# A fourth of the weights' low parts subtracted on GpSimd instead of VectorE, in two passes of a trunk kernel

## The chip, the core and the metric

The kernel runs on one core of a Trainium2 chip. TensorE (PE) multiplies, VectorE (DVE) and ScalarE (ACT) do elementwise work, GpSimd (POOL) is a fourth compute engine, and SyncE (SP) issues the DMAs. Each engine runs its own instructions in order, and they wait for each other by semaphores. The metric is the device time of one execution in microseconds (us), lower is better.

## The reference

A trunk of two layers over 256 tokens of width 2048. Layer 0 mixes with pooling windows, layer 1 with a gated recurrence; each is followed by a SwiGLU feed-forward network (FFN) of hidden width 5632. Norms are modulated by vectors made from a conditioning vector and a large matrix `w_ada`. Cut to what the change touches:

```python
cond = jax.nn.silu(c)
for layer in range(DEPTH):                                   # 2
    mod = cond @ w_ada[layer] + b_ada[layer]                 # 2048 x 12288 each
    sh_m, sc_m, g_m, sh_f, sc_f, g_f = jnp.split(mod[:, None, :], 6, axis=-1)
    h = rms_norm(x, norm_mix_gain[layer]) * (1.0 + sc_m) + sh_m
    ...                                                      # y: pooling or recurrence
    x = x + g_m * y
    h = rms_norm(x, norm_ffn_gain[layer]) * (1.0 + sc_f) + sh_f
    a, b = jnp.split(h @ w_ffn_in[layer], 2, axis=-1)        # 2048 x 11264
    x = x + g_f * ((jax.nn.silu(a) * b) @ w_ffn_out[layer])  # 5632 x 2048
return rms_norm(x, final_gain)
```

## The kernel before

**Products.** Every float32 product is made of three with shorter operands. A weight W is split into a high part (`w_hi`, fp32r) and a low part `w_lo = W - w_hi`; activations are split in the same way into `h_hi` and `h_lo`. TensorE computes hi x hi, hi x lo and lo x hi into one PSUM buffer (lines L548, L549, L550).

**Pairs.** Weights stream from HBM in pairs of blocks, one `raw` tile of 128 x 2 x 512 each (512 KB), 696 pairs in all. A pair n passes through four stages: SP loads it into slot n mod 4 of `raw` (`load_w`, L362); ACT copies it to `w_hi` slot n mod 4 once the load has landed and TensorE has used pair n-4 (`hi`, L859, semaphore `hi_ready`); DVE subtracts (`lo`, L1165, semaphore `lo_ready`); TensorE multiplies two steps of six matmuls of 512 columns (`segment`) and counts `w_used`. SP may load pair n+4 into the slot when the low part of pair n is made.

**Passes of the first FFN.** The product with `w_ffn_in` is cut along its 2048 input features. The first pass takes features 0 to 511 for 9 column blocks of the gate half and 9 of the value half, 18 chunks of two pairs. The second pass takes features 512 to 1023 for the same 18. A pass has 36 pairs. Later passes take the rest. Chunks write alternately to PSUM buffers `prod0` and `prod1`; a chunk can begin when the one two before it has been taken out. In the first pass ACT takes them out to `part_gate` and `part_value` (L957); in the second DVE adds PSUM to these (`add_quarter`, L1464). 

**Beside them.** The vectors from `w_ada` are made in the background: SP loads blocks of 128x1024 into `ada` (L385, L387), DVE multiplies each by a column of the conditioning vector and adds it to `acc` (`fold`, L1211 and L1214). A table of spans (`BEHIND`) says at which steps these loads and folds stand, and code on each engine walks the same steps, so every engine's order is fixed when the program is written: at a step DVE does `lo`, then `add_quarter` or other callbacks, then folds. In the two passes a fold comes at about three of four pairs. SP's order is a pair's load and then the ada loads due.

GpSimd makes constants at the start, then waits (L503) for the first FFN's end before it makes constants for the recurrence.

Of the kernel before, what the change touches and what calls it, by code (L numbers as in the profile page):

```python
# [9 lines left out]
ALU = mybir.AluOpType  # L10
# [30 lines left out]
def build(nc, x, c, norm_mix_gain, norm_ffn_gain, w_ada, b_ada, pool_w, pool_scale, hgrn_w_in,  # L41
# [9 lines left out]
    HG = CH // P  # L51
# [4 lines left out]
    RAW = 4  # L56
    SPL = 4
# [3 lines left out]
    NA = 9  # L61
# [19 lines left out]
    C_M0 = C_A0 + 2 * NA  # L81
    C_B0 = C_M0 + 2 * NA
# [10 lines left out]
    START = [sum(STEPS[:n]) for n in range(len(STEPS) + 1)]  # L93

    def pairs_through(chunk):

        return (START[chunk + 1] + (WFIRST if chunk == C_WOUT else 0)) // 2
# [64 lines left out]
    with ctx:  # L162
        def sb(name, shape, dt=F32, where=ctx):
            return where.enter_context(nc.sbuf_tensor(name, shape, dt))

        def sem(name):
            return ctx.enter_context(nc.semaphore(name))
# [19 lines left out]
        raw = sb("raw", [P, RAW, 2, CH])  # L187
        w_hi = sb("w_hi", [P, SPL, 2, CH], F32R)
        w_lo = sb("w_lo", [P, SPL, 2, CH], F32R)
# [88 lines left out]
        hi_ready = sem("hi_ready")  # L278
# [11 lines left out]
        orstd_ready = sem("orstd_ready")  # L290

        lo_ready = sem("lo_ready")
        unit_summed = sem("unit_summed")
        cols_ready = sem("cols_ready")
        lb_max = sem("lb_max")
# [31 lines left out]
        def evacuated(eng, chunk):  # L327
            eng.wait_ge(prod_free[chunk % 2], chunk // 2 + 1)

        def multiplied(eng, chunk):  # L330
            eng.wait_ge(w_used, pairs_through(chunk))

        def ada_buffer(slot):
            return ada[:, slot] if slot < ADA else ada_head[:, slot - ADA]

# [18 lines left out]
        def _(sp):  # L354
            t = Tally()

            def load_w(src):
                n = t.get("raw")
                slot = n % RAW
                if n >= RAW:  # L360
                    sp.wait_ge(lo_ready, n - RAW + 1)
                sp.dma_start(raw[:, slot], src.rearrange("(a p) n -> p a n", p=P)).then_inc(raw_loaded[slot], 16)  # L362
                t.tick("raw")

# [40 lines left out]
            for src in (c, norm_mix_gain, norm_ffn_gain, hgrn_norm_gain, hgrn_lb):  # L405
                n = src.shape[0] * KD
# [20 lines left out]
            for s in range(0, AHEAD, 2):  # L427
                load_w(w_ffn_in[0, s * P:(s + 2) * P, 0:CH])
# [43 lines left out]
        @block.gpsimd  # L472
        def _(pool):
            pool.memset(ident[:, :], 0.0).then_inc(consts, 1)
            pool.memset(ones[:, :], 1.0).then_inc(consts, 1)
            pool.memset(zero[:, :], 0.0).then_inc(consts, 1)
            pool.wait_ge(consts, 3)
            pool.affine_select(out=ident[:, :], in_=ident[:, :], compare_op=ALU.not_equal, fill=1.0,
                               base=0, pattern=[[-1, P]], channel_multiplier=1).then_inc(consts, 1)
            pool.memset(fours[:, :], 0.0).then_inc(fours_begun, 1)  # L480
            for q in range(P // SQUARE):
                pool.wait_ge(fours_begun, q + 1)
                pool.affine_select(out=fours[:, :], in_=fours[:, :], compare_op=ALU.not_equal, fill=1.0, base=-q * SQUARE,
                                   pattern=[[-1, SQUARE]], channel_multiplier=1).then_inc(fours_begun, 1)

            for n, w in enumerate(WINDOWS):
                pool.memset(band[:, n], 1.0 / w).then_inc(band_begun, 1)
            pool.wait_ge(band_begun, NCH)
            for n, w in enumerate(WINDOWS):
                for at in range(w - 1):  # L490
                    pool.memset(band[:, n, 0, at:at + 1], 1.0 / (at + 1)).then_inc(band_begun, 1)
            pool.wait_ge(band_begun, N_BANDS - 4 * NCH)
            pieces = [(n, w, band[:, n, blk:blk + TB - blk // 2].rearrange("p a c -> p (a c)"), (TB - blk // 2) * P)
                      for n, w in enumerate(WINDOWS) for blk in (0, 2)]
            for _, _, m, cols_of in pieces:
                pool.affine_select(out=m, in_=m, compare_op=ALU.is_ge, fill=0.0, base=0,
                                   pattern=[[1, cols_of]], channel_multiplier=-1).then_inc(band_begun, 1)
            pool.wait_ge(band_begun, N_BANDS - 2 * NCH)
            for _, w, m, cols_of in pieces:
                pool.affine_select(out=m, in_=m, compare_op=ALU.is_ge, fill=0.0, base=w - 1,  # L500
                                   pattern=[[-1, cols_of]], channel_multiplier=1).then_inc(band_begun, 1)

            multiplied(pool, C_H - 1)  # L503
            pool.memset(keep[:, :], 1.0).then_inc(hgrn_consts, 1)
            pool.memset(masks[:, :, :], 1.0).then_inc(hgrn_consts, 1)
            pool.memset(kdec[:, :, :, :], 0.0).then_inc(hgrn_consts, 1)
            pool.wait_ge(hgrn_consts, 3)
            pool.memset(keep[:, :].rearrange("p (n c) -> p n c", c=P)[:, :, 0:1], 0.0).then_inc(hgrn_consts, 1)

            for j, h in enumerate(LEVELS):  # L510
                m = masks[:, j, :].rearrange("p (b o) -> p b o", o=h)
                pool.affine_select(out=m, in_=m, compare_op=ALU.is_ge, fill=0.0, base=0,
                                   pattern=[[-2 * h, P // (2 * h)], [0, h]], channel_multiplier=1).then_inc(hgrn_consts, 1)
            pool.wait_ge(hgrn_consts, 4 + len(LEVELS))
            for j, h in enumerate(LEVELS):
                m = masks[:, j, :].rearrange("p (b o) -> p b o", o=h)
                pool.affine_select(out=m, in_=m, compare_op=ALU.is_ge, fill=0.0, base=h - 1,
                                   pattern=[[2 * h, P // (2 * h)], [0, h]], channel_multiplier=-1).then_inc(hgrn_consts, 1)

        @block.tensor  # L520
        def _(pe):
            t = Tally()
# [9 lines left out]
            def segment(chunk, hi, lo, first, n, after=None, before=None, begin=True, end=True):  # L532

                par = chunk % 2
                if begin and chunk >= 2:
                    evacuated(pe, chunk - 2)
                for s in range(n):
                    if before is not None:
                        before(s)
                    g, k = t.get("step"), first + s  # L540
                    slot = g // 2 % SPL
                    wh, wl = w_hi[:, slot, g % 2], w_lo[:, slot, g % 2]
                    if g % 2 == 0:
                        pe.wait_ge(lo_ready, g // 2 + 1)
                    for tb in range(TB):
                        ts = slice(tb * P, (tb + 1) * P)
                        o = prod[par][:, tb]
                        pe.matmul(o, hi[:, k, ts], wh, start=(begin and s == 0), stop=False)  # L548
                        pe.matmul(o, hi[:, k, ts], wl, start=False, stop=False)  # L549
                        mm = pe.matmul(o, lo[:, k, ts], wh, start=False, stop=(end and s == n - 1))  # L550
                    if g % 2:
                        mm.then_inc(w_used, 1)
                    t.tick("step")
                    if after is not None:
                        after(s)
                    for u, (_, last) in SPAN.items():
                        if g == last + SUM:
                            reduce_unit(u)
# [9 lines left out]
            def multiply_loads(u):  # L568
                pe.wait_ge(unit_taken, u)
                n_rows, _ = folded(u)  # L570
                for k in range(n_rows):
                    n = u * KD + k
                    slot, _ = ada_slot(n)
                    ada_arrived(pe, n)
                    for o in range(2):
                        mm = pe.matmul(modp[:, o], cond_rows[:, k], ada_buffer(slot)[:, o * CH:(o + 1) * CH], start=(k == 0),  # L576
                                       stop=(in_columns(u) and k == n_rows - 1))
                    mm.then_inc(ada_free[slot], 1)
# [579 lines left out]
        def _(dve):  # L1158
            t = Tally()

            def lo():
                n = t.get("pair")
                r, slot = n % RAW, n % SPL
                dve.wait_ge(hi_ready, n + 1)
                dve.tensor_tensor(w_lo[:, slot], raw[:, r], w_hi[:, slot], ALU.subtract).then_inc(lo_ready, 1)  # L1165
                t.tick("pair")

            def ahead():
                for _ in range(AHEAD // 2):
                    lo()  # L1170
# [558 lines left out]
```

## Time and profile before

| | us |
|---|---|
| median of 3 runs | 2229.06 |
| lowest, highest | 2228.64, 2233.13 |
| the profiled execution | 2226.98 |
| its span, first to last instruction | 2225.3 |
| TensorE busy | 2164.4 (97%) |
| DVE busy | 1659.8 (75%) |
| ACT busy | 996.2 (45%) |
| POOL busy | 17.0 (1%) |

The profile is of one execution. Times count from the span's start. Busy is time with an instruction in progress; weight loads (PEld) run beside matmuls. The chain of waits is followed back from the last instruction, at each step to what released it. A window cuts the span, and waits are put down to the instruction that ended them.

### The profile page before, as it was taken

Reading aid. Unit: us, or ns where it says so; the run is one execution under the profiler, and the core shown is the slowest. Engines: PE = TensorE matmul, PEld = TensorE weight load, DVE = VectorE, ACT = ScalarE, POOL = GpSimd, SP = SyncE. Lnnn points to the kernel's source line nnn. Section 1 sums busy time; section 2 is a strip of 40 time slices with the busy share of each in tenths; the row PEclk is TensorE's granted clock in tenths of the full one; section 3 lists DMA queues with packets and bytes.
Section 4 is the critical chain, followed back from the end, with each engine's and each line's share of the span. In section 5 each row is a group of like instructions: output and inputs, shape, how many; then the busy total and the mean of one; then the engine's idle time right before and its main releaser. Section 6 shows DMA issues by size and latency. Waiting matters only on the chain.

```text
span 2225.3 us, 25178 instructions
## 1 busy us (share of the span) xinstructions
PE 2164.4 (97%) x9785; PEld 1757.7 (79%) x9785; DVE 1659.8 (75%) x1695; ACT 996.2 (45%) x1114; POOL 17.0 (1%) x77
## 2 busy tenths in 40 slices
PE   7998999999999999899999999989999999999997
PEld 4556887888888888788888888878888888888886
DVE  5768899999988876578787888667755678456644
ACT  3224544444444444464645455544454444444433
POOL 1000000000000000100000000000000000000000
PEclk9998999999999999999999999999999999999999
DMA  9998998989899886476656664568856687668664
GB/s 384 418 413 306 330 333 307 316 323 315 318 338 315 319 301 231 141 237 203 213 170 208 199 199 141 179 237 305 301 182 188 189 269 254 184 191 292 237 195 147
DMA packets 250067, 574.37 MB, mean 258 GB/s; under 512 B 17526, under 2 KB 17718, under 8 KB 249180
## 3 DMA queue, kind: packets, MB, share of 16 engines
q1 hardware_dynamic: 249948, 572.77, 75.3%
q8 instruction: 77, 1.26, 0.2%
q14 instruction: 42, 0.34, 0.0%
HBM read 570.60 MB, written 2.10 MB: 257 GB/s over the span
## 4 chain that ended last, share of the span: by engine, by line
PE 87%; DVE 3%; issue 2%; ACT 0%; DVEq 0%; ACTq 0%
PE prod L548 27%; PE prod L550 27%; PE prod L549 27%; PE small L786 2%; PE small L619 1%; DVE acc L1214 1%; PE small L760 0%; PE modp L610 0%; DVE part_value L1464 0%; PE small L799 0%; PE small L772 0%; DVE part_gate L1464 0%; PE modp L583 0%; PE small L798 0%; PE small L781 0%
## 5 line engine op out<-in xcount | busy, mean ns | idle before, releaser
L859 ACT ACTIVATE w_hi<-raw 128x1024 fp32r<-128x1024 f32 x696 | 736.4, 1061 | 1026.0 <-PE prod L550 936.2
L1165 DVE TENSOR_TENSOR w_lo<-raw,w_hi 128x1024 fp32r<-128x1024 f32 x696 | 848.4, 1223 | 432.6 <-ACT w_hi L859 430.9
L548 PE MATMUL prod<-w_hi,h_hi 128*128 128x512 f32 x2080 | 823.6, 396 | 5.8 <-issue 2.8
L550 PE MATMUL prod<-w_hi,h_lo 128*128 128x512 f32 x2080 | 811.6, 390 | 0.0
L549 PE MATMUL prod<-w_lo,h_hi 128*128 128x512 f32 x2080 | 810.8, 390 | 0.0
L548 PEld LDWEIGHTS prod<-w_hi,h_hi 128*128 128x128 f32 x2080 | 391.6, 188 | 88.0 <-issue 4.2
L550 PEld LDWEIGHTS prod<-w_hi,h_lo 128*128 128x128 f32 x2080 | 391.2, 188 | 82.9
L549 PEld LDWEIGHTS prod<-w_lo,h_hi 128*128 128x128 f32 x2080 | 391.9, 188 | 79.7 <-issue 1.4
L1214 DVE SCALAR_TENSOR_TENSOR acc<-ada,cond,acc 128x1024 f32<-128x1024 f32 x255 | 326.2, 1279 | 0.4
L548 PE MATMUL prod<-w_hi,g_hi 128*128 128x512 f32 x704 | 275.1, 391 | 0.0
L550 PE MATMUL prod<-w_hi,g_lo 128*128 128x512 f32 x704 | 273.9, 389 | 0.0
L549 PE MATMUL prod<-w_lo,g_hi 128*128 128x512 f32 x704 | 273.9, 389 | 0.0
L549 PEld LDWEIGHTS prod<-w_lo,g_hi 128*128 128x128 f32 x704 | 132.1, 188 | 27.8 <-issue 0.5
L550 PEld LDWEIGHTS prod<-w_hi,g_lo 128*128 128x128 f32 x704 | 132.1, 188 | 27.6
L548 PEld LDWEIGHTS prod<-w_hi,g_hi 128*128 128x128 f32 x704 | 132.1, 188 | 27.6 <-issue 0.5
L576 PE MATMUL modp<-ada,cond_rows 128*128 128x512 f32 x112 | 57.5, 673 | 9.9 <-DMA brows<-in_b_ada 6.5
L619 PE MATMUL small<-ident,tok 128*128 128x128 f32 x272 | 39.8, 295 | 18.9 <-issue 12.2
L786 PEld LDWEIGHTS small<-qdec,kdec 128*128 128x128 f32 x448 | 54.3, 191 | 2.2
L576 PEld LDWEIGHTS modp<-ada,cond_rows 128*128 128x128 f32 x112 | 23.7, 218 | 40.2 <-issue 34.8
L619 PEld LDWEIGHTS small<-ident,tok 128*128 128x128 f32 x272 | 34.9, 152 | 25.1 <-issue 12.9
L786 PE MATMUL small<-qdec,kdec 128*128 128x64 f32 x448 | 53.0, 271 | 0.0
L898 ACT ACTIVATE junk<-xs 128x512 bf16<-128x512 f32 x40 | 25.1, 628 | 43.7 <-DVE xs L1324 43.0
(158 smaller groups left out, 1056.0 us busy)
## 6 DMA issues: line engine op xcount, KB each, us to landing
raw<-in_w_ffn_in SPq DMA_DIRECT2D x352, 512.0 KB, 4.7
ada<-in_w_ada SPq DMA_DIRECT2D x300, 512.0 KB, 6.0
raw<-in_w_ffn_out SPq DMA_DIRECT2D x176, 512.0 KB, 4.4
raw<-in_hgrn_w_in SPq DMA_DIRECT2D x128, 512.0 KB, 3.8
ada_head<-in_w_ada SPq DMA_DIRECT2D x84, 512.0 KB, 14.0
raw<-in_hgrn_w_out SPq DMA_DIRECT2D x32, 512.0 KB, 3.7
raw<-in_pool_w SPq DMA_DIRECT2D x8, 512.0 KB, 15.1
xs<-in_x SPq DMA_DIRECT2D x2, 1024.0 KB, 16.5
```

What stands on the lines that cost most here:

```text
L548: pe.matmul(o, hi[:, k, ts], wh, start=(begin and s == 0), stop=False)
L549: pe.matmul(o, hi[:, k, ts], wl, start=False, stop=False)
L550: mm = pe.matmul(o, lo[:, k, ts], wh, start=False, stop=(end and s == n - 1))
L576: mm = pe.matmul(modp[:, o], cond_rows[:, k], ada_buffer(slot)[:, o * CH:(o + 1) * CH], start=(k == 0), stop=(in_columns(u) and k == n_row ...
L619: mm = pe.transpose(small[half][:, o:o + P], block_of(tb, 2 * half + j), ident[:, :])
L786: mm = pe.matmul(small[b][:, o:o + H], kdec[:, b, hd, blk * P:(blk + 1) * P], qdec[:, b, hd, blk * H:(blk + 1) * H], start=True, stop=True)
L859: act.activation(w_hi[:, slot], raw[:, r], ACT.Copy).then_inc(hi_ready, 1)
L898: act.activation(junk[:, :], xs[:, tb, at * CH:(at + 1) * CH], ACT.Square, accum_out=ssq[:, tb, at:at + 1]).then_inc(squared, 1)
L1165: dve.tensor_tensor(w_lo[:, slot], raw[:, r], w_hi[:, slot], ALU.subtract).then_inc(lo_ready, 1)
L1214: ins = dve.scalar_tensor_tensor(a, ada_buffer(slot), cond[:, k:k + 1], a, ALU.mult, ALU.add)
```

## The change

Among the 72 pairs of the two passes (numbers 8 to 79) those with n mod 4 = 2, 18 pairs (10, 14, ... 78), get their low part from GpSimd. GpSimd waits for the pair's high part, subtracts and counts a semaphore of its own, `pool_lo_ready`. `lo` on DVE skips these pairs. TensorE, before it multiplies a pair, and SP, before it loads over a slot, wait by `low_parts` for the engine that makes the low part of that pair. GpSimd's constants for the recurrence come after the 18.

```diff
--- before.py
+++ after.py
@@ -290,6 +290,7 @@
         orstd_ready = sem("orstd_ready")
 
         lo_ready = sem("lo_ready")
+        pool_lo_ready = sem("pool_lo_ready")
         unit_summed = sem("unit_summed")
         cols_ready = sem("cols_ready")
         lb_max = sem("lb_max")
@@ -330,6 +331,17 @@
         def multiplied(eng, chunk):
             eng.wait_ge(w_used, pairs_through(chunk))
 
+
+        POOL_LO = [n for n in range(START[C_M0] // 2 - HG * NA, START[C_B0] // 2) if n % 4 == 2]
+
+        def low_parts(eng, pair):
+
+            before = sum(n < pair for n in POOL_LO)
+            if pair in POOL_LO:
+                eng.wait_ge(pool_lo_ready, before + 1)
+            else:
+                eng.wait_ge(lo_ready, pair - before + 1)
+
         def ada_buffer(slot):
             return ada[:, slot] if slot < ADA else ada_head[:, slot - ADA]
 
@@ -358,7 +370,7 @@
                 n = t.get("raw")
                 slot = n % RAW
                 if n >= RAW:
-                    sp.wait_ge(lo_ready, n - RAW + 1)
+                    low_parts(sp, n - RAW)
                 sp.dma_start(raw[:, slot], src.rearrange("(a p) n -> p a n", p=P)).then_inc(raw_loaded[slot], 16)
                 t.tick("raw")
 
@@ -500,6 +512,10 @@
                 pool.affine_select(out=m, in_=m, compare_op=ALU.is_ge, fill=0.0, base=w - 1,
                                    pattern=[[-1, cols_of]], channel_multiplier=1).then_inc(band_begun, 1)
 
+            for n in POOL_LO:
+                pool.wait_ge(hi_ready, n + 1)
+                pool.tensor_tensor(w_lo[:, n % SPL], raw[:, n % RAW], w_hi[:, n % SPL], ALU.subtract).then_inc(pool_lo_ready, 1)
+
             multiplied(pool, C_H - 1)
             pool.memset(keep[:, :], 1.0).then_inc(hgrn_consts, 1)
             pool.memset(masks[:, :, :], 1.0).then_inc(hgrn_consts, 1)
@@ -541,7 +557,7 @@
                     slot = g // 2 % SPL
                     wh, wl = w_hi[:, slot, g % 2], w_lo[:, slot, g % 2]
                     if g % 2 == 0:
-                        pe.wait_ge(lo_ready, g // 2 + 1)
+                        low_parts(pe, g // 2)
                     for tb in range(TB):
                         ts = slice(tb * P, (tb + 1) * P)
                         o = prod[par][:, tb]
@@ -1161,6 +1177,9 @@
             def lo():
                 n = t.get("pair")
                 r, slot = n % RAW, n % SPL
+                if n in POOL_LO:
+                    t.tick("pair")
+                    return
                 dve.wait_ge(hi_ready, n + 1)
                 dve.tensor_tensor(w_lo[:, slot], raw[:, r], w_hi[:, slot], ALU.subtract).then_inc(lo_ready, 1)
                 t.tick("pair")
```

The order of DVE in the second pass of the kernel before, where L1165 is a low part, L1214 a fold of an ada block, L1464 the addition of a chunk:

```order
L1464 TENSOR_TENSOR part_gate<-prod0,part_gate 128x1024
L1214 SCALAR_TENSOR_TENSOR acc<-ada,cond,acc 128x1024
L1165 TENSOR_TENSOR w_lo<-raw,w_hi 128x1024
L1214 SCALAR_TENSOR_TENSOR acc<-ada,cond,acc 128x1024
L1165 TENSOR_TENSOR w_lo<-raw,w_hi 128x1024
L1464 TENSOR_TENSOR part_value<-prod1,part_value 128x1024
L1214 SCALAR_TENSOR_TENSOR acc<-ada,cond,acc 128x1024
L1165 TENSOR_TENSOR w_lo<-raw,w_hi 128x1024
L1214 SCALAR_TENSOR_TENSOR acc<-ada,cond,acc 128x1024
L1165 TENSOR_TENSOR w_lo<-raw,w_hi 128x1024
L1464 TENSOR_TENSOR part_gate<-prod0,part_gate 128x1024
```

The same place in the changed kernel, where these lines are L1184, L1233 and L1483:

```order
L1483 TENSOR_TENSOR part_gate<-prod0,part_gate 128x1024
L1233 SCALAR_TENSOR_TENSOR acc<-ada,cond,acc 128x1024
L1184 TENSOR_TENSOR w_lo<-raw,w_hi 128x1024
L1233 SCALAR_TENSOR_TENSOR acc<-ada,cond,acc 128x1024 x2
L1483 TENSOR_TENSOR part_value<-prod1,part_value 128x1024
L1233 SCALAR_TENSOR_TENSOR acc<-ada,cond,acc 128x1024
L1184 TENSOR_TENSOR w_lo<-raw,w_hi 128x1024
L1233 SCALAR_TENSOR_TENSOR acc<-ada,cond,acc 128x1024
L1184 TENSOR_TENSOR w_lo<-raw,w_hi 128x1024
L1483 TENSOR_TENSOR part_gate<-prod0,part_gate 128x1024
```

One low part of four is gone, here the one ahead of an addition to `part_value`; two folds follow each other, and folds and additions keep their order.

The order of GpSimd before, from its last constants of the start to those of the recurrence:

```order
L500 AFFINE_SELECT band<-band 128x256
L500 AFFINE_SELECT band<-band 128x128
L504 MEMSET keep 128x1024 [waits w_used]
L505 MEMSET masks 128x448
L506 MEMSET kdec 128x2048
L508 MEMSET keep 128x8 [waits hgrn_consts]
```

And in the changed kernel:

```order
L512 AFFINE_SELECT band<-band 128x256
L512 AFFINE_SELECT band<-band 128x128
L517 TENSOR_TENSOR w_lo<-raw,w_hi 128x1024 [waits hi_ready] x18
L520 MEMSET keep 128x1024 [waits w_used]
L521 MEMSET masks 128x448
L522 MEMSET kdec 128x2048
L524 MEMSET keep 128x8 [waits hgrn_consts]
```

The 18 subtractions stand between them, each with its wait for a high part.

## Rows read from the trace of the kernel before

**Rows 1.** The page, section 4: the chain that ended last, by engine.
```profile
PE 87%; DVE 3%; issue 2%; ACT 0%; DVEq 0%; ACTq 0%
```

**Rows 2.** The two passes: busy us by engine, clock, DMA share, GB/s.
```profile
184.00:284.00 100.00, 99.70 (x437) 82.26 (x438) 89.55 (x89) 56.10 (x58) 0.00 (x0) 0.98 0.91 331
284.00:389.00 105.00, 101.94 (x452) 82.08 (x451) 102.84 (x106) 42.34 (x45) 0.00 (x0) 1.00 0.90 326
```

**Rows 3.** Waits of the second pass, TensorE's weight loads: total, times, longest.
```profile
PEld prod L548 <- DVE part_value L1464: 3.1, 3, 2.0
PEld prod L548 <- DVE part_gate L1464: 2.5, 3, 1.1
```

**Rows 4.** The chain in the second pass, by line.
```profile
by line: issue 23.8%; DVE acc L1214 23.8%; PE prod L548 9.8%; PE prod L550 9.1%; PE prod L549 9.1%; DVE part_value L1464 7.0%; DVE part_gate L1464 5.8%; DVE w_lo L1165 3.3%; DVE h_lo L1294 1.4%; DVE h_hi L1291 1.3%; ACT feat L928 1.3%; ACT 
```

**Rows 5.** Timeline of DVE in the second pass: start us, us, what.
```profile
300.56 1.22 DVE L1165 TENSOR_TENSOR w_lo<-raw,w_hi 128x1024 fp32r<-128x1024 f32 x1
301.70 1.28 DVE L1214 SCALAR_TENSOR_TENSOR acc<-ada,cond,acc 128x1024 f32<-128x1024 f32 x1
302.89 1.22 DVE L1165 TENSOR_TENSOR w_lo<-raw,w_hi 128x1024 fp32r<-128x1024 f32 x1
304.03 1.22 DVE L1464 TENSOR_TENSOR part_gate<-prod,part_gate 128x1024 f32<-128x1024 f32 x1
...
306.36 1.22 DVE L1165 TENSOR_TENSOR w_lo<-raw,w_hi 128x1024 fp32r<-128x1024 f32 x1
```

**Rows 6.** Groups of GpSimd (POOL) instructions, whole run.
```profile
L506 POOL MEMSET kdec<- 128x2048 f32 x1 | 1.8, 1805 | 0.0
...
L500 POOL TENSOR_SCALAR_AFFINE_SELECT band<-band 128x256 f32<-128x256 f32 x4 | 1.6, 401 | 0.1
...
L500 POOL TENSOR_SCALAR_AFFINE_SELECT band<-band 128x128 f32<-128x128 f32 x4 | 1.2, 294 | 0.0
L504 POOL MEMSET keep<- 128x1024 bf16 x1 | 1.0, 952 | 918.2 <-PE prod L550 918.2
```

**Rows 7.** Timeline at 8.3 us, DVE beside GpSimd.
```profile
8.16 0.16 DVE L1344 TENSOR_TENSOR lbt<-lbt 128x16 f32<-128x16 f32 x1
8.28 0.40 POOL L500 TENSOR_SCALAR_AFFINE_SELECT band<-band 128x256 f32<-128x256 f32 x1
8.36 0.35 DVE L1346 TENSOR_TENSOR lbt<-lbt 128x16 f32<-128x16 f32 x1
```

**Rows 8.** Timeline at 934 us, DVE beside GpSimd.
```profile
933.71 0.66 POOL L512 TENSOR_SCALAR_AFFINE_SELECT masks<-masks 128x64 f32<-128x64 f32 x1
933.85 0.81 DVE L1287 TENSOR_SCALAR tok<-xs,rstd 128x512 f32<-128x512 f32 x1 [0.27 <-ACT rstd L916]
```

**Rows 9.** The line L1287: ns min/median/max.
```profile
L1287 DVE TENSOR_SCALAR tok<-xs,rstd x24: 467/482/806, 173.2 to 1647.5; 128x512 f32<-128x512 f32 x24
```

**Rows 10.** Groups of DVE instructions, second pass: busy, mean ns, idle before, releaser.
```profile
L1165 DVE TENSOR_TENSOR w_lo<-raw,w_hi 128x1024 fp32r<-128x1024 f32 x36 | 43.7, 1218 | 1.3 <-ACT w_hi L859 1.2
L1214 DVE SCALAR_TENSOR_TENSOR acc<-ada,cond,acc 128x1024 f32<-128x1024 f32 x25 | 32.0, 1281 | 0.2
L1464 DVE TENSOR_TENSOR part_gate<-prod,part_gate 128x1024 f32<-128x1024 f32 x9 | 11.0, 1220 | 0.3 <-PE prod L550 0.3
L1464 DVE TENSOR_TENSOR part_value<-prod,part_value 128x1024 f32<-128x1024 f32 x8 | 9.8, 1220 | 0.0
```

**Rows 11.** Waits of DVE in the second pass.
```profile
DVE w_lo L1165 <- ACT w_hi L859: 1.2, 2, 1.0
DVE part_gate L1464 <- PE prod L550: 0.3, 1, 0.3
```

**Rows 12.** Groups of DVE instructions, first pass.
```profile
L1165 DVE TENSOR_TENSOR w_lo<-raw,w_hi 128x1024 fp32r<-128x1024 f32 x36 | 43.9, 1220 | 10.1 <-ACT w_hi L859 9.6
```

**Rows 13.** Timeline of ScalarE (ACT) in the second pass.
```profile
302.70 1.06 ACT L859 ACTIVATE w_hi<-raw 128x1024 fp32r<-128x1024 f32 x1 [1.46 <-DMA raw<-in_w_ffn_in]
```

**Rows 14.** Waits of the DMA-issuing queue (SP) in the second pass.
```profile
SPq L362 <- DVE w_lo L1165: 54.8, 31, 4.4
```


## Prediction, made before the changed kernel ran

> **What bounds the kernel now.** I read the page's chain of waits first. TensorE holds 87% of it and VectorE (DVE) 3% [rows 1], so the kernel is a matmul kernel with some DVE-bound islands. Then I cut the stretch of the change at its passes. The first pass over the first FFN's input weights runs from about 184 to 284 us, the second to about 389 us. Both have 36 pairs of weight blocks, so without stalls they would take the same time. In the first, TensorE issued 438 weight loads in 100 us, 0.228 us each; a pair has 12 matmuls and so takes 2.74 us, and TensorE was idle for 0.3 us. DVE was busy for 89.6 us. In the second DVE was busy for 102.8 of 105 us [rows 2].
>
> The waits of the second pass name the loser: TensorE's weight loads waited 5.6 us, in six waits, for DVE's additions to `part_value` and `part_gate` [rows 3]. That is the most that a faster DVE could give back. The chain of that window agrees: over half of it is DVE lines, or "issue" in between [rows 4].
>
> Why DVE: a matmul chunk here is two pairs, 5.5 us on TensorE. In the same time DVE makes two low parts, folds two ada blocks and adds one chunk. Their pitches, from start to next start, are 1.14 (300.56 to 301.70), 1.19 (301.70 to 302.89) and, for the addition, 306.36 - 304.03 less a fold's 1.19, 1.14 us [rows 5]; 3 x 1.14 + 2 x 1.19 = 5.8 us. DVE loses 0.3 us a chunk until TensorE waits for a free PSUM buffer.
>
> **The change, part by part.** It removes 18 DVE subtractions: 9 in each pass, every fourth pair. Each frees the pitch of 1.14 us, not its 1.22 us, as neighbours overlap. That is 10.3 us of DVE time per pass. Folds, additions and their order stay.
>
> It adds 18 subtractions of 128x1024 on GpSimd, which is idle for 918.2 us before the setup of the recurrence at 929 us [rows 6]. No such instruction exists before, so its time P must be bounded. GpSimd's selects took 294 ns for 128 elements and 401 ns for 256 [rows 6]: 0.84 ns an element over a fixed 0.19 us, reading one operand while writing. One such sweep over 1024 elements is 1.04 us, my lower end. Two operands read in turn give 0.19 + 1.71 = 1.90 us. If the write, at the memset's 1805 ns for 2048 elements or 0.88 ns each [rows 6], came on top, P would be 2.8 us, my upper end. The nearest row is the select, whose write hides beside its read, so P is near 1.9; I take 2.1, a tenth more, because two reads that alternate will hardly run without gaps. That tenth is a choice.
>
> The GPSIMD Engine Reference of the Trainium skill (section 3.1) has a measured 4497 ns for a two-input fp32 `tensor_tensor` of 2048 elements; half of it is an estimate of 2.25 us. By it the sum below would be 1.3 us higher. No run here shows such an instruction yet.
>
> Does it cost DVE anything? The trace has small collisions. At 8.36 us a DVE `TENSOR_TENSOR` on 16 elements, both inputs in SBUF, started inside a GpSimd select that ran from 8.28 to 8.68, and took 0.35 us, ending at 8.71; the same form at 8.16, between selects, took 0.16 [rows 7]. At 933.85 a DVE `TENSOR_SCALAR` of 128x512 started inside a select that ended at 934.37 and took 0.81 us [rows 8], against a median of 482 ns [rows 9]. Each time DVE went on only when the whole GpSimd instruction was over. So a GpSimd instruction that reads SBUF stops DVE's instruction for all of its time, and I expect the same the other way round.
>
> [...]
>
> The additions read one operand from PSUM, and no row shows such an instruction beside a GpSimd select. There are 17 rows of them in the second pass, against 36 low parts and 25 folds [rows 10], 22% of the long ones. If they are not stopped, a block that falls on one costs DVE nothing for its 1.14 us, a credit of 0.22 x 1.14 = 0.25 us per GpSimd instruction; if they are, the credit is zero. I take 0.25, because the collisions shown are with operands in SBUF, and keep the 9 x 0.25 = 2.3 us between the ends for the range. Then each handed-over pair costs DVE P - 0.25 - 1.14 = 0.71 us net instead of saving 1.14. At the lower P of 1.04 it would save 0.1 to 0.35.
>
> Second pass: 9 x 0.71 = 6.4 us more for an engine that is already the bound. DVE's idle time there was 1.2 + 0.3 us [rows 11], of which I let 0.4 be used: +6.0 us. First pass: no additions, so 9 x (2.1 - 1.14) = 8.6 us, against 10.1 us in which DVE sat idle before low parts [rows 12]; TensorE did not wait for it and I cost it at nothing. If that cover were gone (P of 2.8 gives 9 x 1.66 = 15 us) about 5 us would come through.
>
> Waits. GpSimd waits for the high part alone and has nothing else queued until 929 us. TensorE reaches a pair three pairs, 3 x 2.74 = 8.2 us, after ScalarE may begin its high part; less 1.06 us for that [rows 13] 7.1 us are left, against P plus one DVE instruction in progress, 2.1 + 1.3 = 3.4 us. SyncE's in-order queue now waits for GpSimd's semaphore before it refills the slot, and the ada loads stand behind that wait. It waited 54.8 us for low parts before [rows 14]; DVE got to a low part up to 2.6 us after its high part (302.70 + 1.06 = 303.76, its low part at 306.36 [rows 5, 13]), and GpSimd should finish it no later than DVE did, 3.4 us against 3.8 us. TensorE's extra wait replaces another and is free.
>
> Sum against the profiled execution's own 2226.98 us: +6.0, 2233.0 us. That execution is 2.1 us under the median of the runs shown, 2229.06; on the median's footing all values move by 2.1, and the forecast is 2235 us.
>
> **Rivals.**
> No contention at this size (18%). The collisions shown are of 16 and 512 elements, and the 512 one is another kind of instruction; if long subtractions share the ports, DVE has 10.3 us less to do in the second pass and falls under TensorE's pace (5.8 - 0.57 = 5.2 us a chunk against 5.5). At most the 5.6 us of waits go; I take 4, since stops behind clumps (bias additions, turns, normalising) partly stay. 2225 us. This is the other side.
>
> DVE keeps the port (15%). DVE starts its next instruction 0.08 us before the last has ended (1.14 against 1.22 us [rows 5]), so a waiting GpSimd may get in only when idle time comes, or an addition, if that does not need what GpSimd holds. Then the addition hides 1.14 of P, the block is 2.1 - 1.14 = 0.96 and the saving 1.14: 9 x -0.18 = -1.6 us, with up to 4.7 us of delay for GpSimd (two low parts and two folds), 6.8 us in all against the 7.1 us of slack, so a few short TensorE waits. About 2229 us. For it speaks the overlap; the collisions shown are all of a waiting DVE and say nothing of a waiting GpSimd.
>
> A long P (7%). With 2.8 us the second pass costs 9 x 1.41 = 12.7 us and the first 5 us: 2247 us. Above a P of 5.8 us TensorE would even wait for each of the 18 directly. It decides from about P = 2.3, where the first pass's idle time is used up.
>
> **Chances.** Contention with alternation has 60%, its own range 2231 to 2240 us (P from 1.9, +4.6 us, to 2.4, +9). About 0.2%, 4.5 us, is what a measurement of this kernel can tell from no change. Faster by more needs the no-contention case in its better half: 0.12. Within: the rest of that case, nearly all of "DVE keeps the port" and a fourth of the main case: 0.36. Slower: 0.52. The range 2224.5 to 2243 takes in the no-contention value and leaves out the far end of a long P.
>
> **What would show it.** In the second pass the remaining low parts and folds that meet a GpSimd subtraction last 2 to 3.4 us instead of 1.2, and the additions stay at 1.22; GpSimd's rows last 2.1 us, more when they wait. The second pass lasts 111 us instead of 105, with TensorE waiting for additions some 11 us; everything behind 389 us is shifted, not changed. If DVE's means stay at 1.22 and 1.28 us, the contention step is wrong; if they rise and the passes stay as long as before, the claim that DVE bounds the pass is wrong; if TensorE or SyncE waits for GpSimd's low parts, the slack step is.

## The result, and the profile after

The changed kernel took 2237.38 us (median of 6 runs, 2235.43 to 2241.1), the kernel before 2229.12 us in the same comparison (6 runs, 2227.04 to 2233.13). The ratio is 1.0032, with a 95% interval of 1.0018 to 1.0047: slower by 0.3%. The profiled execution has a span of 2233.7 us, 8.4 us more than before.

| | before | after |
|---|---|---|
| span, us | 2225.3 | 2233.7 |
| TensorE, from pair 8 used to pair 43 used | 96.6 | 97.5 |
| from pair 43 used to pair 79 used | 105.4 | 112.1 |
| from pair 79 used to the last | 1820.5 | 1820.6 |
| DVE busy | 1659.8 | 1670.0 |
| POOL busy | 17.0 | 64.8 |

The three stretches are read from the times at which TensorE's matmuls count the semaphore `w_used` in the trace. In the tables below, "first pass" and "second pass" are the first two of them. Of the 8.4 us, 6.7 lie in the second pass, 0.9 in the first and 0.8 before them. The 0.8 is not shown to come from the change: from pair 7 used to pair 8 used it took 38.9 us instead of 38.0, but 38.9 us as well in two of the kernels below in which GpSimd subtracts nothing before pair 8. Behind pair 79 nothing changed.

The same view of the two passes as in [rows 2], of the changed kernel (busy us and instructions of PE, PEld, DVE, ACT, POOL, then granted clock, DMA share, GB/s):

```profile
184.00:284.00 100.00, 99.07 (x430) 81.26 (x431) 92.14 (x77) 54.94 (x57) 23.15 (x9) 0.97 0.90 327
284.00:389.00 105.00, 98.06 (x425) 79.33 (x424) 102.58 (x93) 40.42 (x43) 24.64 (x9) 0.97 0.84 303
```

DVE has 13 instructions fewer than before in the second window (93 against 106) and is busy for as long. What they last is in the groups of the second pass, to be set beside [rows 10]:

```profile
L1233 DVE SCALAR_TENSOR_TENSOR acc<-ada,cond,acc 128x1024 f32<-128x1024 f32 x25 | 42.5, 1701 | 0.2
L1184 DVE TENSOR_TENSOR w_lo<-raw,w_hi 128x1024 fp32r<-128x1024 f32 x27 | 37.1, 1378 | 1.8 <-ACT w_hi L875 1.7
L1483 DVE TENSOR_TENSOR part_gate<-prod,part_gate 128x1024 f32<-128x1024 f32 x8 | 9.7, 1216 | 0.1
L1483 DVE TENSOR_TENSOR part_value<-prod,part_value 128x1024 f32<-128x1024 f32 x8 | 9.7, 1214 | 0.0
```

The mean fold went from 1281 to 1701 ns and the mean low part from 1218 to 1378; the additions stayed at 1.2 us. That is 25 x 0.420 + 27 x 0.160 = 14.8 us of added time for nine GpSimd subtractions, 1.65 us each. The GpSimd line itself, as ns min/median/max and first and last start:

```profile
L517 POOL TENSOR_TENSOR w_lo<-raw,w_hi x18: 2402/2504/3602, 185.0 to 386.0; 128x1024 fp32r<-128x1024 f32 x18
```

The mechanism can be read instruction by instruction. Three cases, from timelines of the changed kernel (start us, us, what). First a fold that starts 0.27 us after GpSimd:

```profile
309.07 3.42 DVE L1233 SCALAR_TENSOR_TENSOR acc<-ada,cond,acc 128x1024 f32<-128x1024 f32 x1
312.42 1.21 DVE L1483 TENSOR_TENSOR part_value<-prod,part_value 128x1024 f32<-128x1024 f32 x1
```

and GpSimd at the same place:

```profile
308.80 2.61 POOL L517 TENSOR_TENSOR w_lo<-raw,w_hi 128x1024 fp32r<-128x1024 f32 x1 [7.67 <-ACT w_hi L875]
```

GpSimd ends at 311.41, the fold at 312.49, 1.08 us later. Each of the 18 GpSimd subtractions has a DVE instruction that it held; the 17 that are low parts or folds (two SBUF operands) end 1.08 or 1.09 us after GpSimd's end, whenever they had started, and the other, a `TENSOR_SCALAR`, 0.55 us after. So the whole instruction is held back, not slowed. Second, an addition inside GpSimd's time:

```profile
298.67 2.47 POOL L517 TENSOR_TENSOR w_lo<-raw,w_hi 128x1024 fp32r<-128x1024 f32 x1 [10.65 <-ACT w_hi L875]
298.79 1.22 DVE L1483 TENSOR_TENSOR part_value<-prod,part_value 128x1024 f32<-128x1024 f32 x1
...
299.92 2.30 DVE L1233 SCALAR_TENSOR_TENSOR acc<-ada,cond,acc 128x1024 f32<-128x1024 f32 x1
```

The addition reads PSUM and one SBUF tensor and takes its usual 1.22 us; only the fold behind it waits, for 2.30 us. Third, a GpSimd subtraction that waits itself:

```profile
275.96 4.63 DVE L1233 SCALAR_TENSOR_TENSOR acc<-ada,cond,acc 128x1024 f32<-128x1024 f32 x2
...
276.14 3.36 POOL L517 TENSOR_TENSOR w_lo<-raw,w_hi 128x1024 fp32r<-128x1024 f32 x1 [10.71 <-ACT w_hi L875]
```

The first of the two folds ran from 275.96 to 277.24. GpSimd began at 276.14 and took 3.36 us instead of 2.40; the second fold then ended 1.08 us behind it. The exclusion goes both ways: GpSimd ends 2.26 us after the fold that it met.

The waits of TensorE's weight loads in the second pass, as in [rows 3]:

```profile
PEld prod L564 <- DVE part_value L1483: 4.3, 2, 2.5
PEld prod L564 <- DVE part_gate L1483: 4.1, 2, 3.9
PEld prod L564 <- DVE w_lo L1184: 0.8, 1, 0.8
```

9.2 us instead of 5.6, in fewer and longer waits, up to 3.9 us. The clock fell too: behind two of the waits the matmuls ran at a pace of 0.43 instead of 0.228 us. Windows around the first (columns as above):

```profile
325.00:333.00 8.00, 5.90 (x19) 4.39 (x18) 7.90 (x8) 2.11 (x2) 0.00 (x0) 0.79 0.87 290
333.00:341.00 8.00, 7.48 (x33) 5.82 (x32) 7.90 (x7) 3.61 (x4) 3.30 (x1) 1.00 0.77 241
```

The same view of the other place:

```profile
371.00:377.00 6.00, 2.87 (x7) 2.19 (x8) 6.00 (x5) 0.00 (x0) 0.86 (x1) 0.72 0.48 158
```

These windows hold waits of 2.5 and 3.9 us; the granted clock is 0.79 and 0.72 of 2.4 GHz, which is a stretch at 1.2 GHz inside each. Over the whole second window it is 0.97, in [rows 2] 1.00. In the half-speed stretches 8 and 5 matmuls cost 0.2 us more each, 2.6 us of TensorE's time. What of it reached the end of the pass is read from DVE, which was behind at the time. After the first stretch DVE never ran idle, so nothing of it is seen there. After the second DVE waited once:

```profile
380.46 1.23 DVE L1184 TENSOR_TENSOR w_lo<-raw,w_hi 128x1024 fp32r<-128x1024 f32 x1 [1.73 <-ACT w_hi L875]
```

ScalarE was late with that high part because its own queue had waited for TensorE's transposes (L635), behind the stop:

```profile
377.55 1.93 ACT L944 ACTIVATE feat<-small,mod,gain 128x256 f32<-128x256 f32 x4 [8.48 <-PE small L635]
379.36 2.02 ACT L875 ACTIVATE w_hi<-raw 128x1024 fp32r<-128x1024 f32 x2
```

So a stop of TensorE came back to DVE as 1.7 us of idle time. How much of this is the stop of 3.9 us and how much the clock behind it is not shown.

SyncE's waits over both passes include GpSimd now:

```profile
SPq L374 <- DVE w_lo L1184: 86.6, 48, 6.5
...
SPq L374 <- POOL w_lo L517: 20.6, 9, 3.4
```

### The profile page after: what moved, and what is told of

Read it like the earlier page. It is cut to its first block, busy times and chain, and to the rows that moved or that the text cites. A ratio compares the mean times of both kernels' runs of the same rounds, so it can differ in the third digit from the quotient of the medians.

```text
span 2233.7 us, 25178 instructions
## 1 busy us (share of the span) xinstructions
PE 2166.5 (97%) x9785; PEld 1760.5 (79%) x9785; DVE 1670.0 (75%) x1677; ACT 996.0 (45%) x1114; POOL 64.8 (3%) x95
## 4 chain that ended last, share of the span: by engine, by line
PE 86%; DVE 4%; issue 2%; ACT 0%; DVEq 0%; ACTq 0%
PE prod L564 27%; PE prod L566 27%; PE prod L565 27%; PE small L802 2%; DVE acc L1233 2%; PE small L635 1%; PE small L776 0%; DVE w_lo L1184 0%; PE modp L626 0%; DVE part_gate L1483 0%; PE small L815 0%; PE small L788 0%; PE small L814 0%; PE modp L599 0%; PE small L797 0%
## 5 line engine op out<-in xcount | busy, mean ns | idle before, releaser
L1184 DVE TENSOR_TENSOR w_lo<-raw,w_hi 128x1024 fp32r<-128x1024 f32 x678 | 831.3, 1230 | 427.6 <-ACT w_hi L875 426.2
L1233 DVE SCALAR_TENSOR_TENSOR acc<-ada,cond,acc 128x1024 f32<-128x1024 f32 x255 | 349.1, 1369 | 3.6 <-DMA ada<-in_w_ada 2.3
L635 PE MATMUL small<-ident,tok 128*128 128x128 f32 x272 | 39.9, 295 | 19.0 <-issue 12.2
L517 POOL TENSOR_TENSOR w_lo<-raw,w_hi 128x1024 fp32r<-128x1024 f32 x18 | 47.8, 2655 | 329.9 <-ACT w_hi L875 329.9
L635 PEld LDWEIGHTS small<-ident,tok 128*128 128x128 f32 x272 | 35.0, 153 | 25.4 <-issue 13.1
```

What stands on the lines that cost most here:

```text
L517: pool.tensor_tensor(w_lo[:, n % SPL], raw[:, n % RAW], w_hi[:, n % SPL], ALU.subtract).then_inc(pool_lo_ready, 1)
L635: mm = pe.transpose(small[half][:, o:o + P], block_of(tb, 2 * half + j), ident[:, :])
L1233: ins = dve.scalar_tensor_tensor(a, ada_buffer(slot), cond[:, k:k + 1], a, ALU.mult, ALU.add)
```

## The experiments

Each run was compared with runs of the kernel before on the same chip. The head of the program, which no edit touches, varied from run to run by up to 6 us (pair 7 was used at 150.7 to 156.8 us), so beside the ratio the table has the passes, which were much steadier: the second pass was 105.4 us in each of the three kernels that left it alone or gave it only writes (before, first pass only, writes added).

| run | median us | before, us | ratio (95%) | first pass | second pass |
|---|---|---|---|---|---|
| before | | | | 96.6 | 105.4 |
| the change | 2237.38 | 2229.12 | 1.0032 (1.0018 to 1.0047) | 97.5 | 112.1 |
| first pass only | 2229.91 | 2229.22 | 1.0004 (0.9995 to 1.0014) | 97.5 | 105.4 |
| second pass only | 2237.25 | 2229.22 | 1.0031 (1.0019 to 1.0043) | 96.8 | 112.9 |
| subtraction added | 2255.14 | 2229.22 | 1.0120 (1.0092 to 1.0147) | 102.8 | 124.5 |
| low parts left out | 2225.30 | 2229.22 | 0.9983 (0.9972 to 0.9993) | 96.6 | 101.7 |
| writes added | 2230.50 | 2230.96 | 1.0003 (0.9992 to 1.0013) | 96.5 | 105.4 |
| copies added | 2233.34 | 2230.96 | 1.0016 (1.0004 to 1.0028) | 96.6 | 110.6 |
| first spreading | 2232.89 | 2230.96 | 1.0014 (1.0002 to 1.0026) | 96.5 | 104.3 |
| two units forward | 2227.55 | 2230.81 | 0.9985 (0.9974 to 0.9996) | 97.0 | 102.2 |
| three units forward | 2227.27 | 2230.81 | 0.9983 (0.9971 to 0.9995) | 96.9 | 101.2 |

### Each pass alone

```diff
-        POOL_LO = [n for n in range(START[C_M0] // 2 - HG * NA, START[C_B0] // 2) if n % 4 == 2]
+        POOL_LO = [... if n % 4 == 2 and n < START[C_M0] // 2]     # first pass only
+        POOL_LO = [... if n % 4 == 2 and n >= START[C_M0] // 2]    # second pass only
```

> GpSimd makes only the 9 low parts of the first pass; DVE makes all of the second. Theory (a GpSimd subtraction holds 2.4 us and stops any DVE instruction with two SBUF inputs until it is over, and this costs only where DVE bounds): DVE loses about 15.7 us and saves 10.3 in the first pass, the net 5.4 us fit into its 10.1 us of idle time; the first pass grows by 0 to 1.2 us, the second stays at 105.4 us, total 2229 to 2231 us. Rival (the cost is the latency of GpSimd's low part, for which SyncE and TensorE wait, the same in both passes): half of the 8 us, total 2233 us.

> GpSimd makes only the 9 low parts of the second pass. Theory: first pass as before the change (96.6 us from pair 8 to 43), second pass about 112 us instead of 105.4, total 2235 to 2237 us. Rival (latency of GpSimd's low part): half of the 8 us, total 2233 us, with SyncE's or TensorE's waits for GpSimd making up the difference.

Measured: with the first pass alone the time is that of before (ratio 1.0004) and the first pass 0.9 us longer; with the second alone nearly the whole loss is there (1.0031) and that pass is 7.5 us longer. The rival, equal halves, is out. The same GpSimd work costs eight times as much where DVE has no idle time. The low parts of GpSimd were late for TensorE in neither: no wait of TensorE for GpSimd is in any of these traces.

### The GpSimd subtraction added, nothing saved

```diff
             def low_parts(eng, pair):
+                eng.wait_ge(lo_ready, pair + 1)
+                if pair in POOL_LO:
+                    eng.wait_ge(pool_lo_ready, sum(n < pair for n in POOL_LO) + 1)
...
-                pool.tensor_tensor(w_lo[:, n % SPL], raw[:, n % RAW], w_hi[:, n % SPL], ALU.subtract)
+                pool.tensor_tensor(scratch, raw[:, n % RAW], w_hi[:, n % SPL], ALU.subtract)
...
-                if n in POOL_LO:
-                    t.tick("pair")
-                    return
```

Here and in the two kernels with another instruction, `scratch` stands for a part of `g_lo` that is not yet in use, and ScalarE waits for all 18 before `g_hi` is first written; that wait stands behind the two passes.

> DVE makes all 72 low parts; the 18 GpSimd subtractions stay as they are but write to a scratch tile, and TensorE and SyncE wait for both. This is the price of the GpSimd instructions without the saving. Theory (whole instructions exclude each other): DVE loses 1.65 to 1.75 us for each, some 15 us in each pass; the second pass grows by 14 to 18 us over before, the first by 5 after its idle time is used, total 2248 to 2254 us. Rival (the two engines share ports without stopping each other, and the 8 us come from late low parts): the instructions finish as late as in the changed kernel, total at most 2237 us.

Measured: the second pass is 19.1 us longer than before and the first 6.3, total 2255.14 us, all three just above what was expected. DVE's groups of the second pass in this run:

```profile
L1180 DVE TENSOR_TENSOR w_lo<-raw,w_hi 128x1024 fp32r<-128x1024 f32 x37 | 51.2, 1388 | 0.3 <-ACT w_hi L873 0.2
L1229 DVE SCALAR_TENSOR_TENSOR acc<-ada,cond,acc 128x1024 f32<-128x1024 f32 x26 | 44.9, 1725 | 0.2
```

37 x 0.170 + 26 x 0.444 = 17.8 us are added to DVE in this window, which also holds a fold that met the last subtraction of the first pass. Taken one by one, the nine held instructions of the second pass last 16.0 us longer than alone, 1.8 us each: without the saved low parts DVE has work waiting at all times, and more of each GpSimd instruction hits it. The pass grew by more than 16.0 us because DVE came into it late: its first addition stands 9.9 us behind the use of pair 43, in the kernel before 5.5. The rival allowed 2237 us at most and is out. GpSimd's own instructions did last longer than in the changed kernel (median 2.86 us against 2.50, at most 4.65), but TensorE waited for none of them.

### The low parts left out

GpSimd does nothing, and TensorE multiplies for these 18 pairs what an earlier pair left in the low buffer; that part of the product is left out.

```diff
             if pair in POOL_LO:
-                eng.wait_ge(pool_lo_ready, before + 1)
+                eng.wait_ge(hi_ready, pair + 1)
...
-            for n in POOL_LO:
-                pool.wait_ge(hi_ready, n + 1)
-                pool.tensor_tensor(w_lo[:, n % SPL], ...)
```

> The 18 low parts are made by nobody (TensorE multiplies what an earlier pair left in the buffer, so that part of the product is left out); TensorE and SyncE wait for the high part alone. This is the most that handing them over could save if GpSimd were free. Theory: DVE's 10.3 us per pass come off and the second pass falls to 101 to 102 us, as most of the 5.4 us of TensorE waits for additions go; total 2224 to 2226 us. Rival (DVE does not bound the second pass; its waits sit elsewhere): within 1 us of 2229.

Measured: 0.9983, second pass 101.7 us, 3.7 less. A GpSimd that cost DVE nothing would have been worth that and no more. The no-contention rival had put 4 us on it; its size was right and its premise wrong.

### Which GpSimd instructions stop DVE

Both kernels are the one with the subtraction added, with another instruction in its place:

```diff
+                pool.memset(g_lo[:, 36:44].bitcast(F32), 0.0)    # 128x2048: writes only
+                pool.tensor_copy(scratch, raw[:, n % RAW])       # 128x1024: one operand read
```

> DVE makes all 72 low parts; in place of each of the 18 subtractions GpSimd fills 128x2048 of a scratch tile with zeros (about 1.8 us), which writes SBUF and reads nothing. Theory (it is the read of the second operand through something shared that stops DVE): no DVE instruction gets longer, 2229 us. Rival (any GpSimd access of SBUF stops DVE): 18 x about 1.1 us more of DVE time, second pass 8 to 10 us longer, 2238 us or more.

> DVE makes all 72 low parts; in place of each of the 18 subtractions GpSimd copies the pair's 128x1024 raw tile to scratch, one operand read. Theory (a GpSimd instruction that reads SBUF stops a DVE instruction with two SBUF inputs for its own duration): the copy holds about 1.0 to 1.3 us, DVE loses 0.4 to 1.0 us each, the second pass grows by 3 to 9 us, total 2232 to 2240 us. Rival (only a GpSimd instruction with two operands collides): DVE's instructions stay at 1.22 and 1.28 us, 2229 us.

Measured: 18 memsets of 1.8 us change nothing (1.0003, second pass 105.4 us). A DVE low part that lies wholly inside one, from the timeline at 310 us:

```profile
310.38 1.82 POOL L515 MEMSET g_lo<- 128x2048 f32 x1 [9.31 <-ACT w_hi L873]
310.45 1.21 DVE L1180 TENSOR_TENSOR w_lo<-raw,w_hi 128x1024 fp32r<-128x1024 f32 x1
```

18 copies make the second pass 5.3 us longer. The copy needs 1.04 us when it meets nothing, and 0.9 us behind a DVE instruction that it had to wait for (225.37 to 226.28 below), and every fold or low part that ran into one was held:

```profile
224.15 1.22 DVE L1180 TENSOR_TENSOR w_lo<-raw,w_hi 128x1024 fp32r<-128x1024 f32 x1 [0.28 <-ACT w_hi L873]
...
224.18 2.10 POOL L515 CAST g_lo<-raw 128x1024 fp32r<-128x1024 f32 x1 [8.38 <-ACT w_hi L873]
...
225.29 2.06 DVE L1229 SCALAR_TENSOR_TENSOR acc<-ada,cond,acc 128x1024 f32<-128x1024 f32 x1
```

The copy arrives just after a low part has begun at 224.15, waits until 225.37, and ends at 226.28; the fold behind it ends at 227.35, again 1.07 us after. So one operand read is enough, and the rival that two are needed is out.

### Spreading DVE's own work

If DVE's density bounds the second pass, work can be taken out of it without GpSimd. These are the kernel before with other entries in the table of spans.

```diff
-              ((0, SC_F, 1), A0 + 80, A0 + 108, A0 + 116), ((0, G_F, 0), A0 + 118, A0 + 156, None),
+              ((0, SC_F, 1), A0 + 76, A0 + 108, A0 + 116), ((0, G_F, 0), A0 + 124, A0 + 160, None),   # first spreading
```

> The kernel before, with no GpSimd work, but two background units spread more thinly: the folds of one (0, SC_F, 1) start 4 steps earlier (A0+76 instead of A0+80) and those of the next (0, G_F, 0) run from A0+124 to A0+160 instead of A0+118 to A0+156. If the second pass is bound by DVE's density of work there, as the theory says, its TensorE waits shrink from 5.4 us to 2 to 3 us and the time to 2225 to 2228 us; if not, 2229 us as before.

Measured: 1.0014, slower and not faster as expected, although the second pass is 1.1 us shorter. The loss is behind it: pairs 80 to 119 took 118.0 us instead of 114.6. DVE's longest wait there, in this run:

```profile
DVE acc L1211 <- PE modp L610: 7.4, 1, 7.4
```

In the kernel before:

```profile
DVE acc L1211 <- PE modp L610: 3.7, 1, 3.7
```

A unit that ends at A0+160 is summed by TensorE at A0+163, and the next unit's first fold stands at A0+162 on DVE's in-order queue, ahead of low parts. My edit had moved the end towards it. Moving units forward avoids that:

```diff
-              ((0, SH_F, 1), A0 + 40, A0 + 72, None), ((0, SC_F, 1), A0 + 80, A0 + 108, A0 + 116),
-              ((0, G_F, 0), A0 + 118, A0 + 156, None),
+              ((0, SH_F, 1), A0 + 36, A0 + 66, None), ((0, SC_F, 1), A0 + 70, A0 + 108, A0 + 116),    # two, three units
+              ((0, G_F, 0), A0 + 113, A0 + 153, None),                                                # three units
```

> The kernel before with two background units moved forward: (0, SH_F, 1) from A0+40..72 to A0+36..66 and (0, SC_F, 1) from A0+80..108 to A0+70..108, so that its 16 folds stand in 39 steps instead of 29, part of them in the first pass where DVE sits idle for 10 us. A chunk of the second pass then has 1.64 folds in place of 2.2, 3 x 1.14 + 1.64 x 1.19 = 5.4 us of DVE against 5.45 us of TensorE. Theory (the second pass is bound by DVE, and work that is moved to idle time is worth what leaving out low parts was): second pass 102 to 103.5 us, total 2226 to 2227.5 us. Rival (loads of the ada blocks come too early and collide with the weights in the first pass): the first pass grows by as much, 2229 us.

> As the run with two units moved forward, and the folds of (0, G_F, 0) from A0+118..156 to A0+113..153, which also ends them earlier before the next unit begins at A0+162. Theory: the second stretch of TensorE waits (365 to 385 us before) shrinks too, second pass 101.5 to 103 us, total 2225 to 2227 us. Rival: the shorter gap behind the unit before delays DVE at its first fold (it waits until that unit's sum is out), and the gain stays at that of the other run or less.

Measured: 0.9985 and 0.9983, second pass 102.2 and 101.2 us, the totals 2227.55 and 2227.27 us just above what was expected. The waits for additions with three units forward:

```profile
PEld prod L548 <- DVE part_gate L1464: 1.3, 2, 0.8
PEld prod L548 <- DVE part_value L1464: 0.5, 1, 0.5
```

1.8 us of the 5.6 are left. Of the 4.2 us gained in the second pass 0.4 is lost in the first and 0.4 behind it. The two medians are alike, and so the third unit is not shown to help the total. Both are faster than the kernel before and than the changed one.

## Why the prediction was right

**The bound.** Right. The second pass was DVE's: leaving 10.3 us of DVE work out gave 3.7 us, adding 16.0 us cost 19.1, and the first pass, where DVE had idle time, moved by 0.9 us for the same change. The sum of 5.8 us a chunk, however, holds only where folds stand two to a chunk; over the pass there are 25 folds to 18 chunks [rows 10], and DVE's bias additions, turns and normalising fill up the rest.

**Contention.** Right, with more to it than was claimed. The collision at 8.36 us [rows 7] was an instance of what all 18 subtractions show. That at 934 us [rows 8] is of another kind: a `TENSOR_SCALAR`, which reads one SBUF tensor, is held even by a GpSimd instruction that reads nothing (last section). That GpSimd waits in turn was expected and is shown.

**P.** Mis-sized: 2.1 us was chosen from selects, the subtraction lasts 2.40 us when nothing is in its way. The estimate from the GPSIMD Engine Reference of the Trainium skill (section 3.1), 2.25 us, was nearer, and still short.

**The credit for additions.** That they run on was half a guess and is shown by the 1.22 us beside a subtraction. Stream transposes of `acc` (1.24 us beside one) run on as well. The rule of "SBUF — State Buffer" in the Trainium skill (section "Who interferes with whom") is that a DVE instruction with two SBUF inputs contends with a GpSimd instruction that reads SBUF and not with one that only writes it. The traces agree: low parts and folds were held by subtractions (up to 3.43 us) and by copies (2.06 us) and not by memsets (1.21 and 1.28 us), and an addition with one operand in PSUM was not held.

**Net cost for each pair.** Forecast 0.71 us of DVE time, measured 1.65 - 1.14 = 0.51 in the second pass. The longer P would have made it 1.01. Taken one by one, the nine held instructions last 1.67 us longer than alone, in two groups. Five cost DVE 2.12 to 2.16 us, about the 2.1 forecast and less than GpSimd's 2.40, since a held instruction ends 1.08 us after GpSimd and alone takes 1.22 to 1.28. Four cost 1.02 to 1.18 us, because an addition (three times) or a stream transpose ran on beside GpSimd first. So the credit was about 0.47 us and not 0.25, and the P that was too short did not count. Two errors of opposite sign.

**The sum.** Forecast +6.0 in the second pass, measured +6.7. By DVE's net cost alone it is 9 x 0.51 = 4.6 us. The rest has a term that the prediction did not have. From its first addition to its last (290.9 to 394.1 us before, 292.6 to 402.2 after) DVE was busy for 4.8 us longer and idle for 1.5 us longer, nearly all of it the one wait of 1.7 us above; the prediction had let DVE's idle time shrink by 0.4. The total was met because a net cost that was too high and an idle time left out came to nearly the same: this part is luck. Half the clock for 13 matmuls does not explain it: with the second pass alone TensorE had one such stretch instead of two, and the pass was 0.8 us longer still.

**First pass.** Costed at nothing, with 8.6 us of net DVE time against 10.1 us of idle. Measured: 30 folds 0.421 us longer, 25 low parts 0.040 longer and one `TENSOR_SCALAR` 2.1 us longer, 15.7 us, less 10.3 saved, is 5.4 us; 0.9 us came through. It is one wait of TensorE, at 266.7 us, for a low part that stood on DVE behind a fold held until 266.52:

```profile
PEld prod L564 <- DVE w_lo L1184: 1.0, 1, 1.0
```

The kernel with the first pass alone has the same wait of 1.0 us. So idle time summed over the pass does not cover a delay at one place. The prediction had also claimed that SyncE's wait for GpSimd would be free. In its total that holds: SyncE waited nine times for GpSimd, 20.6 us, but its waits for low parts of both engines are 107.2 us against 108.9 before (180 to 395 us). DVE's folds of the first pass now waited 2.3 us for ada loads, for which they had not waited before; that SyncE's queue is the reason is likely and not shown:

```profile
L1233 DVE SCALAR_TENSOR_TENSOR acc<-ada,cond,acc 128x1024 f32<-128x1024 f32 x30 | 51.0, 1701 | 3.3 <-DMA ada<-in_w_ada 2.3 <-DVE acc L1233 0.5
```

**Waits.** TensorE never waited for a GpSimd low part, as forecast, and in the second pass its waits grew to 9.2 us where some 11 had been forecast. "DVE keeps the port" was seen in part. With copies, at 202 us:

```profile
202.38 1.28 DVE L1229 SCALAR_TENSOR_TENSOR acc<-ada,cond,acc 128x1024 f32<-128x1024 f32 x1
203.57 1.22 DVE L1180 TENSOR_TENSOR w_lo<-raw,w_hi 128x1024 fp32r<-128x1024 f32 x1
204.71 2.06 DVE L1229 SCALAR_TENSOR_TENSOR acc<-ada,cond,acc 128x1024 f32<-128x1024 f32 x1
```

and GpSimd's copy there:

```profile
202.42 3.27 POOL L515 CAST g_lo<-raw 128x1024 fp32r<-128x1024 f32 x1 [10.04 <-ACT w_hi L873]
```

The copy arrived at 202.42, but a fold and a low part that follow without a gap went first, and it ran from about 204.8 on. It delays GpSimd but does not spare DVE, since the next fold is held all the same.

## What to carry to other kernels

Before handing elementwise work to an idle GpSimd, compare what it holds with what it saves: here an SBUF-reading instruction of 2.4 us stops every DVE instruction with two SBUF operands that meets it, and saves one of 1.14. Of what met it in these traces it left alone only DVE's additions and copies out of PSUM and its stream transposes; else it can pay where DVE is idle, and there DVE needs no help. When an engine bounds one stretch by a few per cent, look first for its own background work that can stand a few steps earlier, and check where each moved piece ends against who waits for its result.

## What the runs showed of the hardware that was not expected

- A GpSimd `MEMSET` leaves `TENSOR_TENSOR` and `SCALAR_TENSOR_TENSOR` on DVE alone, but held a DVE `TENSOR_SCALAR` that reads one SBUF tensor. Beside a subtraction, in the changed kernel, the same instruction took 2.87 us. The median of this line is 0.75 us. Beside the memset, the one instance seen, it took 2.10 us and ended 0.55 us after it:

```profile
188.94 1.80 POOL L515 MEMSET g_lo<- 128x2048 f32 x1 [178.22 <-ACT w_hi L873]
189.19 2.10 DVE L1226 TENSOR_SCALAR acc<-ada,cond 128x1024 f32<-128x1024 f32 x1
```

- A held DVE instruction of 1024 elements ends 1.07 to 1.09 us after the release, less than its 1.22 to 1.28 us alone: so part of its time passes while it is held.
- TensorE fell to 1.2 GHz after stops of 2.5 us (8 matmuls at 0.43 us) and 3.9 us (5 matmuls, then transposes), 3.4 us each time, and it began to do so 1.5 us into the work behind the first of them. The stop of 1.8 us at 340 us, and those of 2.0 us or less in the kernel before, had no such stretch. But the length of the stop does not decide it. With the second pass alone the clock stayed at 2.4 GHz behind stops of 2.9 and 3.1 us and fell behind one of 3.9; with the copies it stayed behind 2.6 and 2.8 us and fell behind 2.4. What decides it is not shown. In the kernel with the second pass alone, around the stops of 2.9 and 3.9 us:

```profile
329.00:341.00 12.00, 9.52 (x41) 7.20 (x40) 11.90 (x11) 3.82 (x5) 0.50 (x2) 1.00 0.87 294
...
375.00:385.00 10.00, 6.51 (x26) 5.10 (x25) 8.90 (x6) 2.24 (x5) 2.04 (x1) 0.83 0.59 206
```
